# A hybrid attention block on one core: x loaded and split in whole rows, the values' weight tile finished ahead of the keys', and the third product's high half ahead of the keys' copies

## The reference

```python
h = jnp.einsum('bsd,de->bse', x, w_in) + b_in            # x: 1 x 1024 x 1024, float32
q_a, k_a, v_a, gate_a, q_b, k_b, v_b, gate_b, mg_a, mg_b = jnp.split(h, split_points, axis=-1)
q_a = rope(q_a.reshape(B, S, SWA_Q_HEADS, HEAD_DIM), positions)
k_a = rope(k_a.reshape(B, S, SWA_KV_HEADS, HEAD_DIM), positions)      # 128 columns
v_a = v_a.reshape(B, S, SWA_KV_HEADS, HEAD_DIM)                       # 128 columns
o_a = swa_sink_attention(q_a, k_a, v_a, sinks) * jax.nn.silu(gate_a)
y_a = jnp.einsum('bse,ed->bsd', o_a, w_up_a)
o_b = stick_breaking_attention(...) * jax.nn.silu(gate_b)
y_b = jnp.einsum('bse,ed->bsd', o_b, w_up_b)
merged = jax.nn.sigmoid(mg_a) * y_a + jax.nn.sigmoid(mg_b) * y_b
sub = jnp.einsum('bsd,de->bse', merged, w_out)
return layer_norm(DEEPNORM_ALPHA * x + sub, ln_g, ln_b)
```

## Time and profile before

| | us |
|---|---|
| median of 3 runs | 708.12 (707.87 to 708.31) |
| the profiled execution, its device time | 707.53 |
| its span in the profile | 705.8 |
| TensorE busy | 693.9 (98%) |
| VectorE busy | 574.6 (81%) |
| ScalarE busy | 461.3 (65%) |

### The profile page before, as it was taken

How to read it: one execution, slowest core, us unless ns; L and a number is a source line. 1 busy time by engine, 2 the same in 40 slices (tenths; PEclk the granted TensorE clock), 3 DMA queues, 4 the chain that set the end, 5 groups by cost and what they waited for, 6 DMA issues and landing times.

```text
span 705.8 us, 10856 instructions
## 1 busy us (share of the span) xinstructions
PE 693.9 (98%) x3938; PEld 567.6 (80%) x3938; DVE 574.6 (81%) x794; ACT 461.3 (65%) x797; POOL 109.4 (16%) x140
## 2 busy tenths in 40 slices
PE   8999999999999999999999999999999999999995
PEld 7888877777888888888878888888888888888884
DVE  6998788775888997898799885676869977899876
ACT  7954377775876866676777765666459855658432
POOL 0000000000554333233213220000000000000266
PEclk9999999999999999999999999999999999999998
DMA  9235423221669855661203122879433876688376
GB/s 322 96 95 123 112 79 103 75 64 59 236 209 214 189 165 113 142 158 52 90 17 119 61 75 66 312 264 346 144 120 120 255 224 202 197 335 337 120 120 119
DMA packets 56084, 110.31 MB, mean 156 GB/s; under 512 B 13008, under 2 KB 17616, under 8 KB 55504
## 3 DMA queue, kind: packets, MB, share of 16 engines
q1 hardware_dynamic: 48672, 88.64, 37.8%
q0 software_dynamic: 7072, 20.45, 13.6%
q10 hardware_dynamic: 288, 0.52, 0.2%
HBM read 86.53 MB, written 41.42 MB: 181 GB/s over the span
## 4 chain that ended last, share of the span: by engine, by line
PE 96%; DVE 2%; DMA 1%; issue 0%; ACT 0%; SPq 0%; POOL 0%; DVEq 0%; POOLq 0%; ACTq 0%
PE ps L273 26%; PE ps L275 26%; PE ps L274 26%; PE ps L2327 5%; PE ps L2339 5%; PE ps L2312 4%; PE ps L2256 1%; PE ps L2268 1%; PE ps L2237 1%; DVE keep L1801 1%; DMA xr<-in_xt 1%; PE ps L2291 0%; DVE o_t L2118 0%; PE ps L2225 0%; DVE o_t L2127 0%
## 5 line engine op out<-in xcount | busy, mean ns | idle before, releaser
L273 PE MATMUL ps<-x_hi,w_hi 128*128 128x512 f32 x432 | 173.4, 401 | 1.3 <-DVE x_lo L1708 1.1
L275 PE MATMUL ps<-x_hi,w_lo 128*128 128x512 f32 x432 | 168.7, 391 | 0.0
L274 PE MATMUL ps<-x_lo,w_hi 128*128 128x512 f32 x432 | 168.4, 390 | 0.0
L1591 DVE TENSOR_TENSOR w_lo<-raw,w_hi 128x512 fp32r<-128x512 f32 x142 | 96.6, 693 | 45.6 <-ACT w_hi L1035 45.0
L273 PE MATMUL ps<-t_ops,w_hi 128*128 128x512 f32 x288 | 115.1, 399 | 0.0
L275 PE MATMUL ps<-t_ops,w_lo 128*128 128x512 f32 x288 | 112.5, 390 | 0.0
L274 PE MATMUL ps<-t_ops,w_hi 128*128 128x512 f32 x288 | 112.3, 390 | 0.0
L1801 DVE TENSOR_TENSOR_SCAN keep<-keep 128x895 f32<-128x895 f32 (+4 forms) x64 | 86.4, 1380 | 14.9 <-POOL keep L931 14.9
L273 PEld LDWEIGHTS ps<-x_hi,w_hi 128*128 128x128 f32 x432 | 81.2, 188 | 18.0 <-issue 2.9
L275 PEld LDWEIGHTS ps<-x_hi,w_lo 128*128 128x128 f32 x432 | 81.1, 188 | 17.4
L274 PEld LDWEIGHTS ps<-x_lo,w_hi 128*128 128x128 f32 x432 | 81.3, 188 | 15.2
(11 more groups left out here) (246 smaller groups left out, 1174.0 us busy)
## 6 DMA issues: line engine op xcount, KB each, us to landing
raw<-in_w SPq DMA_DIRECT2D x51, 256.0 KB, 2.9
raw<-in_w SPq DMA_DIRECT2D x20, 512.0 KB, 4.1
sig_m<-sig_d SPq DMA_DIRECT2D x16, 512.0 KB, 5.0
sig_d<-sig_m SPq DMA_DIRECT2D x28, 256.0 KB, 3.6
up_sum_d<-in_w POOLq DMA_DIRECT2D x6, 1024.0 KB, 10.5
out_sum_t_d<-in_w POOLq DMA_DIRECT2D x6, 1024.0 KB, 10.4
o_t<-o_d SPq DMA_DIRECT2D x8, 512.0 KB, 6.3
xr<-in_xt SPq DMA_DIRECT2D x14, 256.0 KB, 5.6
```

Of the source, the lines that this page charges most:

```text
L273: pe.matmul(out, w_hi, x_hi, start=first, stop=False, skip_group_check=goes_on)
L274: pe.matmul(out, w_hi, x_lo, start=False, stop=False, skip_group_check=goes_on)
L275: return pe.matmul(out, w_lo, x_hi, start=False, stop=last, skip_group_check=goes_on)
L1591: dve.tensor_tensor(ring_slot(w_lo, q), part_of(q), ring_slot(w_hi, q).bitcast(F32), ALU.subtract).then_inc(part_lo, 1)
```

## The change

Three things. x is cut in nine pieces instead of 16: block 0 in two halves, blocks 1 to 7 whole (1024 tokens, 512 KB); transfers, high copies and low subtractions all go by these pieces, and ACT's queue now issues block 0's second half and block 2. TensorE does block 0 for all four banks, then blocks 1 to 5 for all four, then blocks 6 and 7 of the values' tile, then blocks 6 and 7 of the keys' tile; parts 0 and 1 go to the ring slot of the values' tile, parts 2 and 3 to that of the keys'. In ACT's list the sums come first, then both values' copies, parts 0 and 1, `sum_hi(2)`, part 2, and only then both groups of keys' copies.

```diff
 def halves_done(n, h):
-    return 2 * h + n + 1
-BY_SCALAR = ((0, 1), (0, 3))
+    return h + 1 if n == V_A else h + 3
+X_PIECES = ((0, slice(0, HALF)), (0, slice(HALF, SEQ))) + tuple((k, slice(0, SEQ)) for k in range(1, KT))
+def x_piece(k, h):
+    return h if k == 0 else k + 1
+BY_SCALAR = (1, 3)
@@ ring
-            return t[:, q // 2 % 2, half(q % 2)]
+            return t[:, (q // 2 + 1) % 2, half(q % 2)]
@@ SP
-            for h in range(2):
-                for k in range(KT):
-                    if h == 0 and k < 2:
-                        sp.dma_start(raw[:, k, first_piece(0)], w[k][:, first_piece(0)]).then_inc(first_in[k][0], 16)
...
-                    if (h, k) not in BY_SCALAR:
-                        sp.dma_start(xr[:, k, half(h)], xt[k][:, half(h)]).then_inc(x_in[KT * h + k], 16)
-                if h == 0:
-                    for dst, src in ((bias_c, bias), (sink_c, sinks)):
-                        sp.dma_start(dst[:], src).then_inc(const_in, 16)
+            for i, (k, at) in enumerate(X_PIECES):
+                if i < 2:
+                    sp.dma_start(raw[:, i, first_piece(0)], w[i][:, first_piece(0)]).then_inc(first_in[i][0], 16)
+                if k == 2:
+                    for n in (K_A, V_A):
+                        sp.dma_start(raw[:, n, first_piece(1)], w[n][:, first_piece(1)]).then_inc(first_in[n][1], 16)
+                if k == 4:
+                    for n in (K_A, V_A):
+                        sp.dma_start(raw[:, n, half(1)], w[n][:, half(1)]).then_inc(raw_in[n], 16)
+                if i not in BY_SCALAR:
+                    sp.dma_start(xr[:, k, at], xt[k][:, at]).then_inc(x_in[i], 16)
+            for dst, src in ((bias_c, bias), (sink_c, sinks)):
+                sp.dma_start(dst[:], src).then_inc(const_in, 16)
@@ ACT, part_high
-                    act.wait_ge(half_done, (3, 3, 4, 4)[q])
+                    act.wait_ge(half_done, (2, 2, 4, 4)[q])
@@ ACT, its list
-            for h, k in BY_SCALAR:
-                act.dma_start(xr[:, k, half(h)], xt[k][:, half(h)]).then_inc(x_in[KT * h + k], 16)
...
+            for i in BY_SCALAR:
+                k, at = X_PIECES[i]
+                act.dma_start(xr[:, k, at], xt[k][:, at]).then_inc(x_in[i], 16)
+            for i, (k, at) in enumerate(X_PIECES):
+                if i < 2:
+                    first_weights_hi(i, 0)
+                if k in (2, 4):
+                    for n in (K_A, V_A):
+                        first_weights_hi(n, k // 2)
+                act.wait_ge(x_in[i], 16)
+                act.activation(x_hi[:, k, at], xr[:, k, at], ACT.Copy).then_inc(x_hi_done, 1)
             act.wait_ge(const_in, 32)
 
-            value_half(0)
-            keys_swap(0)
             sum_hi(1)
             sum_hi(3)
+            value_half(0)
+            value_half(1)
             part_high(0)
             part_high(1)
             sum_hi(2)
             part_high(2)
-            value_half(1)
+            keys_swap(0)
             keys_swap(1)
             for q in range(WINDOW_1):
                 after(q)
@@ DVE
+                dve.wait_ge(x_hi_done, i + 1)
+                dve.tensor_tensor(x_lo[:, k, at], xr[:, k, at], x_hi[:, k, at].bitcast(F32),
+                                  ALU.subtract).then_inc(x_lo_done, 1)
@@ PE
-                if n == K_A:
-                    pe.wait_ge(x_lo_done, KT * h + k + 1)
+                pe.wait_ge(x_lo_done, x_piece(k, h) + 1)
...
-            for k in range(KT):
-                for n in (K_A, V_A):
-                    last = first_block(n, 0, k)
-                    if k == KT - 1:
-                        last.then_inc(half_done, 1)
-            for n in (K_A, V_A):
-                for k in range(KT):
-                    last = first_block(n, 1, k)
-                last.then_inc(half_done, 1)
+            for h in range(2):
+                for n in (K_A, V_A):
+                    first_block(n, h, 0)
+            for k in range(1, KT - 2):
+                for n in (K_A, V_A):
+                    for h in range(2):
+                        first_block(n, h, k)
+            for n in (V_A, K_A):
+                for k in (KT - 2, KT - 1):
+                    for h in range(2):
+                        last = first_block(n, h, k)
+                        if k == KT - 1:
+                            last.then_inc(half_done, 1)
```

More of the change, by code:

```diff
@@ L621, in build @@
         out_done = ((sem("out_done0"), 0), (sem("out_done1"), 0), (up_summed, 16 * 8), (wo_summed[0], 16 * 8))
-        out_set, out_last = (x_in[KT + 2], 16), (t_hi[4], 2)
+        out_set, out_last = (x_in[KT + 3], 0), (t_hi[4], 2)
         stage_in, stage_out = ([(x_in[4 * e + u], 16) for u in range(len(STAGED))] for e in range(2))
-        b11_in = [(x_in[KT + p], 16) for p in range(2)]
+        b11_in = [(x_in[KT + 1 + p], 0) for p in range(2)]
         stage_hi, stage_lo = ((t_lo[t], 2) for t in (1, 2))
@@ L1515, in sum_raw @@
                     if t == 1:
-                        dve.wait_ge(x_lo_done, 2 * KT)
+                        dve.wait_ge(x_lo_done, len(X_PIECES))
                         dve.tensor_tensor(o, x_raw(0, 1, i), o, ALU.subtract).then_inc(t_raw[t], 1)
@@ L1699, in _ @@
             dve.memset(eps_c[:], LN_EPS).then_inc(eps_set, 1)
-            for h in range(2):
-                for k in range(KT):
[L1702 to L1709, removed]
+            for i, (k, at) in enumerate(X_PIECES):
+                if i < 2:
+                    first_weights_lo(i, 0)
+                if k in (2, 4):
+                    for n in (K_A, V_A):
+                        first_weights_lo(n, k // 2)
+                dve.wait_ge(x_hi_done, i + 1)
+                dve.tensor_tensor(x_lo[:, k, at], xr[:, k, at], x_hi[:, k, at].bitcast(F32),
+                                  ALU.subtract).then_inc(x_lo_done, 1)
             dve.wait_ge(const_in, 32)
```

7 lines of the change are left out of this document (removed).

## The result

The change makes the kernel slower: 711.64 us (median of 6 runs, 711.24 to 714.26) against 708.00 (6 runs, 707.43 to 709.50), ratio 1.0057, 95% interval 1.0045 to 1.0068. That is 3.2 to 4.8 us. The profiled execution took 711.44, its span 709.7 against 705.8: 3.9 us more.

The account below looks back on a forecast made before the run. The prediction took TensorE, busy 693.9 of 705.8 us, as the bound. A start 0.46 later and a stall of 2.69 at product 2 add 3.15 to the median of 708.12: 711.3 us, range 710.2 to 713.4.

Parts of the forecast that it names:

- The sum: Whole kernel: late start of 0.46 plus stall of 2.69 at product 2, 3.15 us slower, median 711.3.
- The keys' copies: ACT's list ahead of product 0's reading: the copies delay it, so product 2 waits 2.69 us (2.4 to 3.1).
- the term for part 2: ACT's part 2 starts at T + 1.14 instead of T + 0.26, T being product 0's start: 0.88 us later.
- the margin of 0.29: Before the change, product 0's bank was read by 34.21 and product 2 started at 34.50: 0.29 us to spare.
- The start: First or thirteenth matmul: block 0 or block 1 comes late, about 0.5 us lost (nothing to 1.0).
- The form with equal numbers of packets: Loading: queues share packet by packet, so ACT's larger rows make block 0 and the first matmul 0.56 us late.
- The reckoning by bytes for block 1: Loading: block 1 lands at about 8.0 and is ready at 10.48 against 10.02, a loss of 0.46 us.
- The later blocks and products: Blocks 2 to 7 cost nothing, with a microsecond or more to spare each; nothing else becomes late behind product 2.
- The clock's fall: Rival: TensorE's clock drops to half rate in the stall, up to 2.2 us more, 713.5; chance 0.10.
- No stall: Rival: the keys' copies don't stand in product 2's way, no change, 708.1 to 708.6 us; chance 0.05.
- faster: Rival: the start gains over 4 us to pay for the stall, or over 1.4 without it; chance 0.03.

Follow-up runs that it names:

- copies spread: Changed kernel with the keys' eight copies placed one behind each reading of products 1 to 8: 710.58 us, ratio 1.0032 to the kernel before.
- one transfer by ACT's queue: Changed kernel with block 2 issued by SP, leaving ACT's queue only block 0's second half: 712.69 us, ratio 1.0065 to the kernel before.
- halves again: Changed kernel with x in sixteen half pieces again, the orders of tiles and ACT's list as changed: 712.74 us, ratio 1.0065 to the kernel before.
- keys moved: Kernel before, with only the first group of keys' copies moved directly ahead of the second: 712.15 us, ratio 1.0051.
- a sum on GpSimd: Kernel before with an earlier start, second group of keys' copies spread, and one of VectorE's sums of x's blocks moved to GpSimd: 712.10 us, ratio 1.0051.
- transposes in both gaps: Changed kernel with 28 instead of 22 transposes at the start and 24 ahead of product 2: 711.88 us, ratio 1.0051 to the kernel before.
- copies twice: Changed kernel with each of the keys' eight copies made twice, the second behind a semaphore: 720.00 us, ratio 1.0164 to the kernel before.

## Why the prediction was right

**The sum.** 3.15 us were predicted, the trace has 3.9, and the difference of the medians is 3.6. Slower, within the range (710.2 to 713.4), one new wait at product 2 and a late start: as put. That the median comes within 0.4 of the 711.3 named owes something to chance: both terms are too small against this pair of profiles, and the profile of the kernel before is one of its quicker runs.

**The keys' copies.** Predicted 2.69, measured 3.03. The mechanism is shown from four sides: the wait ends with `qa<-ps` behind the block of copies; with the copies spread it is gone to the hundredth; with the copies doubled it grows by 0.71 each; with the copies alone moved in the old kernel it is 2.49 where 2.53 were counted (in part by luck: `qa<-ps` began 0.13 sooner against product 0 than counted, and the hand-over named below adds 0.09). What was mis-sized is the term for part 2, put at T + 1.14, when ACT is free of `sum_hi(2)`. It started at T + 1.38, released by DVE's `w_x`: DVE's low parts 0 and 1 and the weight sum stand one behind another from T - 1.28 to T + 1.34 (28.62 to 31.24), as DVE's timeline after the change shows.

```profile
28.62 1.29 DVE L1596 TENSOR_TENSOR w_lo<-raw,w_hi 128x512 fp32r<-128x512 f32 x2 [2.35 <-ACT w_hi L1040]
29.83 0.69 DVE L1585 TENSOR_TENSOR raw<-raw 128x512 f32<-128x512 f32 x1
30.55 0.69 DVE L1587 TENSOR_TENSOR w_x<-raw 128x512 f32<-128x512 f32 x1
```

The prediction had the low parts' times and didn't follow DVE's queue to the next item. That is 0.24 of the 0.34 missing; the last 0.09 is the hand-over from the end of the copy to the matmul (38.28 to 38.37), which the margin of 0.29 (34.21 to 34.50) holds too: only 0.20 of it could be used up.

**The start.** Predicted 0.46 to 0.56, measured 0.84 at product 0: 0.59 for the first matmul, and 0.23 at the thirteenth (0.12 of waiting, and 0.11 more to the next matmul, as behind each stop). The prediction had the two as alternatives (both together as its bound of 1.0); here both came. Much of it is chance. With the nine pieces block 0's copy started at 6.14 to 6.61 in six profiled kernels, with the old loading at 5.68 and 5.93: later with the new one in every trace, by 0.2 to 0.9. But the kernel with only the keys' copies moved was itself 0.64 late at product 0. So against the one old profile the new loading costs 0.8, against the other 0.2, and its true price is not settled.

The form with equal numbers of packets is borne out in part. From 4 to 5 us the changed kernel's queues have these numbers (packets, MB, share), in answer to the earlier trace rows:

```profile
q10 hardware_dynamic: 51, 0.20, 52.7%
q1 hardware_dynamic: 55, 0.11, 45.6%
```

Nearly equal numbers, and nearly twice the bytes for ACT's queue (q10), whose rows are larger; from 5 to 6 us it is 66 against 123. With ACT's second transfer gone, block 0's copy started 0.9 earlier, with it halved 0.4 earlier. The reckoning by bytes for block 1 has a slip: two pieces of 128 KB, 0.26 MB, take 1.09 us at 0.24 MB in a microsecond and 0.66 at 0.40, which is 0.4 more and not 0.2. Rightly summed it gives 7.8 for block 1 and a loss of 0.2 to 0.3 by that form. The copy of block 1 started at 8.33, so the form is off by half a microsecond, and the kernel with one transfer by ACT's queue shows that it is not general.

**The later blocks and products** cost nothing, as said: no wait of L280 for `x_lo` beyond the thirteenth, none of products 3 to 6.

**The rivals.** The clock's fall had 1 chance in 10. It did not happen in the profiled execution, where a stall of 3.0 us left the clock up, but most likely in one of the six runs (0.992) and perhaps in a second (0.995), and by trace in four of the variants (copies spread, halves again, keys moved, a sum on GpSimd), behind idle stretches of 1.9 to 2.9 us, with 1.6 us lost each time. It deserved more: not as a case instead of the sum, but as something that is added to it in some runs. Each of these falls came behind an idle stretch of TensorE, none out of steady work; the kernel with transposes in both gaps fits that and does not prove it, and certain it is only for the stall of 8.7 us, within which the granted clock went to 0.50. Why an idle stretch of 1.9 us brings it in one run and one of 2.9 us doesn't in another stays open. "No stall" and "faster" are excluded by the trace.

## What to carry to other kernels

Where TensorE is busy from end to end, the order of another engine's list counts from both sides: a piece of work that stood in an idle place costs its full length once it stands between a result and the reading that frees that result's bank. Write down for each reader of an output bank what stands ahead of it and its margin (here 0.29 us, 0.09 of them the hand-over), and follow each item to the engine that feeds it, here DVE's weight sum. A stall on TensorE costs more than its length in some runs, through the clock; compare traces product by product before trusting a difference of medians of a microsecond, and two profiles of one kernel, where there are two, before giving a term of half a microsecond a cause.

## What the runs showed of the hardware

- The granted clock went to 0.50 after TensorE had been idle for 1.9, 2.3, 2.6 and 2.9 us in four profiled runs, 0.3 to 1.4 us after work had resumed, for eight matmuls 0.43 apart each time (1.6 us lost), and held behind 2.9 us of idleness in the changed kernel and in the one with one transfer by ACT's queue. In the stall of 8.7 us it fell to 0.50 while TensorE was idle, and was still down when work resumed.
- In one profiled run (copies twice) the first matmuls were 0.43 apart up to 14.2 us, while the clock's row read 1.00: at the start of a run the steps have to be read, not the row.
- A copy by ScalarE of 32 partitions by 512 takes as long (0.68) as one of 128 by 512 (0.69), and eight in a row 5.6 us.
- Two float32 subtractions on VectorE took 5.39 instead of 1.29 us while GpSimd subtracted.
- From 4 to 6 us SP's queue alone (one transfer by ACT's queue) kept the DMA engines 0.63 to 0.71 busy at 153 to 213 GB/s, both queues together (the changed kernel) 0.98 to 1.01 at 307 to 354. From 6 to 7 us SP's queue alone reached 0.98 at 350.
